# RWKV-7 chunk stage: the chunk output formed channel-major with 64 moving columns, its group norm taken by two products with a matrix of 1/64

## The chip, the core and the metric

The kernel runs on one core of one Trainium2 chip. The metric is the device time in microseconds (us) of one execution. TensorE is called PE below (PEld for its weight loads), VectorE DVE, ScalarE ACT, SyncE SP.

## What is computed

One decoder block on 2,064 tokens (16 meta tokens and 2,048 of the sequence) with 1,024 channels. Two branches start from one projection: an RWKV-7 time mixing on 512 channels (8 heads of 64) and an S5 state space model. Gates merge them, an output projection and a gated MLP with a causal convolution follow. The change lies in the RWKV branch, whose state S of each head runs over the tokens:

```python
def _rwkv7_step(S, inp):
    r_t, w_t, k_t, v_t, kk_t, b_t = inp
    sa = jnp.einsum('bhvk,bhk->bhv', S, -kk_t)
    S = S * w_t[:, :, None, :] + sa[..., None] * b_t[:, :, None, :] + v_t[..., None] * k_t[:, :, None, :]
    y = jnp.einsum('bhvk,bhk->bhv', S, r_t)
    return S, y
...
    mean = jnp.mean(y, axis=-1, keepdims=True)
    var = jnp.mean(jnp.square(y - mean), axis=-1, keepdims=True)
    y = ((y - mean) * lax.rsqrt(var + GN_EPS)).reshape(bsz, t_len, RWKV_WIDTH)
    y = y * ln_g.astype(f32) + ln_b.astype(f32)
```

The mean and the variance go over the 64 channels of a head, for each token.

## The kernel before

`hybrid_block` runs the stages one after the other: `norm_transpose` and `in_projection`, `rwkv_prepare`, `rwkv_chunks`, `branch_mix`, `token_projection`, `ffn_up` and `token_projection` again. The change is in `rwkv_chunks` alone (lines 999 to 1459) and in one table of masks that `lay_out` makes.

`rwkv_chunks` cuts the tokens into 33 chunks of 64 and turns the recurrence inside a chunk into matrix products. The 8 heads are 4 pairs (PAIRS); a pair fills the 128 partitions. Everything is float32, and each float32 product is two instructions on PE. The operands of a chunk are "roles" (A, B, K, R, V), loaded channel-major: the tile `roles` holds them block-diagonally, one head's 64 tokens in one half of the columns and the other's in the other half, with zeros elsewhere; the tile `pairs_ar` holds A and R compactly, 64 columns each.

The engines work through a software pipeline that is written out by hand. `steps` calls `step(c, ...)` for c = -1 to 32; the loop of the program holds two of these steps. In step c, PE, DVE and ACT finish chunk c (function names with `main_`), prepare chunk n = c + 1, and normalize chunk c - 1. In PE's order a step is:

- `grams_of` (L1122): the products of B and K with A and R, 128 columns each, into PSUM banks 0 and 1. DVE masks them (`mask_grams`, L1287 to L1297) into `l_t` and into three block-diagonal tiles `grams`.
- `turn_toks` (L1131): K, V and B are transposed; ACT copies them out (L1380).
- `main_u` (L1193): `u` of chunk c, in bank 5; ACT copies it (L1398). `turn_x1`, `main_m` (L1201, L1202) and on DVE `state` (L1313, L1315) update the state `m`.
- Five levels l = 0 to 4 of a triangular inverse. A level is `lx` (L1150) on PE, a masked copy `q` on DVE (L1302), `xq` (L1163, and L1165 in the last level) on PE, an addition into `x` on DVE (L1306, L1308), `turn_x` (L1172) on PE and a copy `x_t` on ACT (L1389), each in two halves of two pairs. Each waits for the one before it.

Into the waits of the levels the PE program puts other products, by the table `between`, whose keys are (level, place): place 0 is behind `lx`, 1 behind `xq`, 2 behind `turn_x`.

```python
between = {(0, 0): (ys, (0,)), (1, 0): (ys, (1,)), (1, 2): (ys, (2,)), (2, 0): (ys, (3,)),
           (2, 1): (ws, (0,)), (2, 2): (ws, (1,)), (3, 0): (ws, (2,)), (3, 1): (ws, (3,))}
```

`ys` is `main_y`: three products for each pair (L1212 to L1214), with block-diagonal R, or masked grams, as the stationary operand and the state, the tokens of V, or u as the moving one, so that y comes out with tokens on the partitions. `ws` is `main_w` for the next chunk (L1183, L1184). ACT copies y out of bank 7 (L1405). The norm of chunk c - 1 is on DVE behind levels 1, 2 and 3: `norm_mean` (a sum over the free axis, a scaling, a subtraction: L1323, L1325, L1327), `norm_squares` (L1331) and `norm_divide` (a reciprocal of 4 numbers in each partition, L1335, and two multiplications into the block-diagonal `y_bd`, L1340). ACT squares (L1409) and takes the root (L1413). In level 4, behind `lx`, PE transposes `y_bd` (`turn_y`, L1224), and ACT copies the result into `y_all` (L1419), which is channel-major. After the last chunk ACT applies the gain and bias (L1459), DVE adds the bonus and multiplies the gate (L1365, L1368), and the result is stored.

SP loads (`load_chunk`): for chunk c + 2, once `main_w` has released the buffers, A and R into `pairs_ar` (L1083), then B, K, A and V into `roles` (L1076), and once y is done R into `roles`.

## Time and profile before

| what | value |
|---|---|
| median of 3 runs | 4137.09 us (4135.92 to 4138.92) |
| the profiled execution: time | 4135.23 us |
| the profiled execution: span of the trace | 4133.5 us |
| mean granted TensorE clock | 0.957 of full speed |
| busy in the span: PE, PEld | 91%, 85% |
| busy in the span: DVE, ACT | 43%, 27% |

The span goes from the first to the last instruction of the trace; the execution's own time is 1.7 us longer. Matmuls overlap in PE's pipeline, so the busy time of PE says that something was in it, not that it was at its peak. Shares over the whole span mix eight stages; the change touches one, which lasts from about 1145 to 2040 us, and the rows quoted below are mostly of that stage. A row of the timeline gives the start, the time that the group took, the engine, the line, what is written and read, how many instructions, and in brackets the idle time of the engine before the group with what ended it. Successive instructions in a group of n on PE start (group time less the time of one) / (n - 1) apart.

### The profile page before, as it was taken

The numbers are of one execution on the slowest core, as the hardware profiler recorded it, in microseconds if no ns is written. First come the engines' busy times: TensorE is split into PE (matmuls) and PEld (weight loads), VectorE is DVE, ScalarE is ACT, GpSimd is POOL, SyncE is SP. The second block draws the span as 40 slices with busy tenths as digits, with TensorE's granted clock in tenths as the row PEclk, the third lists the DMA queues.
The fourth block names the chain that finished last, engine by engine and source line by source line (L and its number), as shares of the span: only waits on it lengthen the run. The fifth ranks groups of instructions, "written<-read, shape, count | busy, mean of one in ns | idle before, by whom it ended". The sixth has DMA issues, their size and how long they took to land. (4 is left out here: it accounts for less than half of the span.)

```text
span 4133.5 us, 61709 instructions
## 1 busy us (share of the span) xinstructions
PE 3778.9 (91%) x23380; PEld 3518.3 (85%) x23380; DVE 1784.3 (43%) x3099; ACT 1107.5 (27%) x1757; POOL 0.2 (0%) x4
## 2 busy tenths in 40 slices
PE   6999999995579999999499898999999999889899
PEld 6999999994468888888489887999999999878687
DVE  6556522224856666666554344322222222211233
ACT  5211133335523333333331133211111111111211
POOL 0000000000000000000000000000000000000000
PEclk8999999997689999999799999999999999999999
DMA  5333333434531111111443343111111111121333
GB/s 141 99 111 124 135 116 125 126 113 165 216 109 36 36 36 36 36 36 36 147 150 115 122 133 107 43 61 41 41 52 49 41 41 51 65 88 49 111 115 96
DMA packets 304699, 366.30 MB, mean 89 GB/s; under 512 B 167872, under 2 KB 250688, under 8 KB 292336
## 3 DMA queue, kind: packets, MB, share of 16 engines
q1 hardware_dynamic: 304624, 365.29, 28.2%
q8 instruction: 49, 0.80, 0.1%
q14 instruction: 26, 0.21, 0.0%
HBM read 225.97 MB, written 139.23 MB: 88 GB/s over the span
## 5 line engine op out<-in xcount | busy, mean ns | idle before, releaser
L2006 PE MATMUL psum<-h_hi,up_w_hi 128*128 128x344 f32 x2112 | 675.8, 320 | 15.2 <-DVE up_w_lo L2050 15.2
L2006 PE MATMUL psum<-h_lo,up_w_hi 128*128 128x344 f32 x2112 | 676.7, 320 | 0.0
L2006 PE MATMUL psum<-h_hi,up_w_lo 128*128 128x344 f32 x2112 | 674.5, 319 | 0.0
L434 PE MATMUL psum<-x_hi,proj_w_hi 128*128 128x344 f32 x1632 | 534.9, 328 | 9.3 <-DVE proj_w_lo L521 8.3
L434 PE MATMUL psum<-x_lo,proj_w_hi 128*128 128x344 f32 x1632 | 524.8, 322 | 0.0
L434 PE MATMUL psum<-x_hi,proj_w_lo 128*128 128x344 f32 x1632 | 523.7, 321 | 0.0
L2006 PEld LDWEIGHTS psum<-h_hi,up_w_hi 128*128 128x128 f32 x2112 | 397.7, 188 | 15.3 <-issue 15.3
L2006 PEld LDWEIGHTS psum<-h_hi,up_w_lo 128*128 128x128 f32 x2112 | 397.8, 188 | 0.0
L2006 PEld LDWEIGHTS psum<-h_lo,up_w_hi 128*128 128x128 f32 x2112 | 397.2, 188 | 0.0
L434 PEld LDWEIGHTS psum<-x_hi,proj_w_hi 128*128 128x128 f32 x1632 | 309.5, 190 | 11.0 <-issue 8.4
L1800 PE MATMUL psum<-down_w_hi,down_a_hi 128*128 128x512 f32 x704 | 278.8, 396 | 41.6 <-DVE down_w_lo L1920 30.2
L434 PEld LDWEIGHTS psum<-x_lo,proj_w_hi 128*128 128x128 f32 x1632 | 309.2, 189 | 1.4
L434 PEld LDWEIGHTS psum<-x_hi,proj_w_lo 128*128 128x128 f32 x1632 | 309.1, 189 | 0.0
L1800 PE MATMUL psum<-down_w_lo,down_a_hi 128*128 128x512 f32 x704 | 276.6, 393 | 0.0
L1800 PE MATMUL psum<-down_w_hi,down_a_lo 128*128 128x512 f32 x704 | 276.5, 393 | 0.0
L1581 PE MATMUL psum<-mix_y_hi,mix_w_hi 128*128 128x344 f32 x576 | 186.6, 324 | 61.3 <-DVE mix_y_lo L1634 61.3
L1389 ACT ACTIVATE chunk_x_t<-psum 128x256 f32<-128x256 f32 x264 | 95.0, 384 | 459.4 <-PE psum L1172 455.3
L2067 DVE TENSOR_SCALAR up_hidden<-up_a_pre,cols_sb 128x2048 f32<-128x2048 f32 x22 | 29.6, 1347 | 420.5 <-ACT up_a_pre L2035 420.5
L1800 PEld LDWEIGHTS psum<-down_w_hi,down_a_hi 128*128 128x128 f32 x704 | 133.9, 190 | 75.4 <-issue 20.3
L1302 DVE TENSOR_TENSOR chunk_q<-psum,chunk_masks 128x256 f32<-128x256 f32 x330 | 137.0, 423 | 122.8 <-PE psum L1150 119.9
L2077 DVE TENSOR_TENSOR up_hidden<-up_hidden,psum 128x328 f32<-128x328 f32 (+1 forms) x132 | 65.4, 509 | 288.8 <-PE psum L2006 243.1
L1150 PE MATMUL psum<-chunk_x,chunk_l_t 128*128 128x128 f32 x1320 | 181.4, 280 | 8.7 <-ACT chunk_x_t L1389 6.5
(290 smaller groups left out, 6231.1 us busy)
## 6 DMA issues: line engine op xcount, KB each, us to landing
up_weight<-in_w_up_tiles SPq DMA_DIRECT2D x22, 1024.0 KB, 4.9
scratch_hidden<-up_hidden SPq DMA_DIRECT2D x22, 1024.0 KB, 3.9
down_a_raw<-scratch_hidden SPq DMA_DIRECT2D x32, 704.0 KB, 5.0
proj_area<-scratch_s_tab SPq DMA_DIRECT2D x32, 608.5 KB, 3.7
scratch_s_tab<-proj_area SPq DMA_DIRECT2D x16, 1089.0 KB, 4.3
proj_weight<-in_w_in_tiles SPq DMA_DIRECT2D x34, 512.0 KB, 4.7
scratch_gates<-proj_mixed SPq DMA_DIRECT2D x16, 1032.0 KB, 4.4
mix_gate<-scratch_gates SPq DMA_DIRECT2D x32, 516.0 KB, 4.9
```

The lines of the kernel that those rows point to most:

```text
L434: mm = nc.tensor.matmul(psum[:, bank(v, n), 0:N_TOK], w[:, v, k, :], x[:, k, cols], start=(k == 0 and w is w_hi and x is x_hi), stop=(k == ...
L1150: mm = T_.matmul(half_bank(h)[:, n, :], l_t[:, 2 * h + j, :], x[:, 2 * h + j, :], start=True, stop=True)
L1302: V.tensor_tensor(q[:, js, :], half_bank(h), wide(3 + l, 2), ALU.mult).then_inc(q_ready, 1)
L1389: A.activation(x_t[:, v, js, :], half_bank(h), ACT.Copy).then_inc(xt_ready, 1)
L1581: mm = nc.tensor.matmul(psum[:, b, 0:N_TOK], w[:, u, part, k, :], y[:, src, k, cols], start=(k == 0 and w is w_hi and y is y_hi), stop=(k ...
L1800: mm = nc.tensor.matmul(psum[0:n, 2 * u + h, :], a[:, u, k, 0:n], w[:, k, h * HALF:(h + 1) * HALF], start=(k == 0 and a is a_hi and w is w ...
L2006: mm = nc.tensor.matmul(psum[:, bank(u, part, n), 0:N_TOK], w[:, u, part, k, :], y[:, k, block_cols(n)], start=(k == 0 and w is w_hi and y ...
L2067: nc.vector.tensor_scalar(out, tap(2), weight_of(2), conv_b[:, bass.ds(m, 1)], ALU.mult, ALU.add).then_inc(tap_done, 1)
L2077: nc.vector.tensor_tensor(cols, cols, psum[:, bank(u, 1, n), skip:N_TOK], ALU.mult).then_inc(b_used, 1)
```

## The change

- y is formed channel-major: the state, the tokens of V, and u are the stationary operands, 128 columns each; the moving operands are R and the masked grams, compact, 64 columns each. y comes out with channels on the partitions and 4 x 64 = 256 tokens on the free axis.
- R is held in `pairs_ar` alone. The block-diagonal load of R goes, and `pairs_ar` is now loaded after the four other roles and after the wait for y.
- The two masked grams that belong to R are kept in compact form (`gram_r`), made by one instruction on 128 partitions each in place of two on 64.
- The mean over a head is a product of y with a constant matrix that has 1/64 inside each head's block (`y_mean`, 256 moving columns, in bank 5), put behind `xq` of level 0; the variance is the same product of the squares (`y_var`), put behind `turn_x` and `main_w` of level 2. DVE subtracts the mean behind level 1. ACT takes the root of all 256 columns. DVE takes the reciprocal of all 256 columns and multiplies straight into `y_all` behind level 3.
- The sums over the free axis, the scaling, `turn_y` and the copy behind it go.

The diff, cut to its core:

```diff
+        gram_a = sb("gram_a", [P, 2, PAIRS, P])
+        gram_r = sb("gram_r", [P, 2, 2, PAIRS, S])
         toks = sb("toks", [P, 2, 3, PAIRS, P])
         pairs_ar = sb("pairs_ar", [P, 2, PAIRS, 2, S])
         l_t = sb("l_t", [P, PAIRS, P])
@@ -1027,10 +1029,9 @@
         w = sb("w", [P, PAIRS, P])
...
-        MASKED = 9
+        MASKED = 7
+        PLACE = {ROLE_A: 0, ROLE_B: 1, ROLE_K: 2, ROLE_V: 3}
+        incl = masks[:, MASK_INCL, 0:S].unsqueeze(1).broadcast_to([P, PAIRS, S])
+        head_mean = masks[:, MASK_MEAN, :]
+        y_bank = psum[:, 7, 0:PAIRS * S].rearrange("p (j c) -> p j c", j=PAIRS)
+        mean_bank = psum[:, 5, 0:PAIRS * S].rearrange("p (j c) -> p j c", j=PAIRS)
+        var_bank = psum[:, 5, PAIRS * S:2 * PAIRS * S].rearrange("p (j c) -> p j c", j=PAIRS)
...
                 if not isinstance(c, int) or c >= 2:
                     sp.wait_ge(w_done, c - 1)
-                for q, r in enumerate((ROLE_A, ROLE_R)):
-                    sp.dma_start(pairs_ar[:, v, :, q, S - n:S], prep[r][:, :, bass.ds(t0, n)].rearrange("j p t -> p j t")).then_inc(ar_loaded[v], 16)
                 for r in (ROLE_B, ROLE_K, ROLE_A, ROLE_V):
                     load(r, v, t0, n, roles_loaded)
                 if not isinstance(c, int) or c >= 2:
                     sp.wait_ge(y_done, c - 1)
-                load(ROLE_R, v, t0, n, r_loaded)
+                for q, r in enumerate((ROLE_A, ROLE_R)):
+                    sp.dma_start(pairs_ar[:, v, :, q, S - n:S], prep[r][:, :, bass.ds(t0, n)].rearrange("j p t -> p j t")).then_inc(ar_loaded[v], 16)
...
-                at(pe, masked, MASKED, c, 3)
-                at(pe, masked, MASKED, c, MASKED - 4)
+                at(pe, masked, MASKED, c, 4)
...
-                done(pe, y_flat, 2, c)
+                at(pe, std_done, 1, c, 1)
...
-            def main_y(c, v, k, pairs):
+            def main_y(c, v, pairs):
                 if pairs[0] == 0:
                     at(pe, u_ready, 1, c, 1)
-                    pe.wait_ge(r_loaded[v], 32 * k + 32)
-                    done(pe, y_ready, 2, c)
+                    done(pe, y_ready, 1, c)
                 for j in pairs:
-                    T_.matmul(bank(7)[:, j, :], R(v, ROLE_R, j), m[:, v, j, :], start=True, stop=False)
-                    T_.matmul(bank(7)[:, j, :], grams[:, v, 2, j, :], toks[:, v, 2, j, :], start=False, stop=False)
-                    mm = T_.matmul(bank(7)[:, j, :], grams[:, v, 1, j, :], u[:, j, :], start=False, stop=True)
+                    T_.matmul(y_bank[:, j, :], m[:, v, j, :], pairs_ar[:, v, j, 1, :], start=True, stop=False)
+                    T_.matmul(y_bank[:, j, :], toks[:, v, 2, j, :], gram_r[:, v, 1, j, :], start=False, stop=False)
+                    mm = T_.matmul(y_bank[:, j, :], u[:, j, :], gram_r[:, v, 0, j, :], start=False, stop=True)
                 if pairs[-1] == PAIRS - 1:
                     mm.then_inc(y_done, 1)
 
-            def turn_y(c):
-                at(pe, normed, 2, c, 2)
+            def y_mean(c):
+                at(pe, y_ready, 1, c, 1)
                 at(pe, u_ready, 1, c, 2 if not isinstance(c, int) or c < NC_ - 1 else 1)
-                if isinstance(c, int) and c == NC_ - 1:
-                    at(pe, y_flat, 2, c, 2)
-                for j in range(PAIRS):
-                    mm = T_.transpose(bank(5)[:, j, :], y_bd[:, j].rearrange("p h c -> p (h c)"), ident)
-                mm.then_inc(y_turned, 1)
+                at(pe, std_done, 1, c, 2)
+                T_.matmul(mean_bank, head_mean, y[:], start=True, stop=True).then_inc(mean_done, 1)
+
+            def y_var(c):
+                at(pe, sq_ready, 1, c, 1)
+                T_.matmul(var_bank, head_mean, y_sq[:], start=True, stop=True).then_inc(var_done, 1)
...
+                    norm = main and not (isinstance(c, int) and c == 0)
+                    mean, var = (lambda: norm and y_mean(c - 1)), (lambda: norm and y_var(c - 1))
+                    between = {(0, 0): (ys, (0,)), (0, 1): (mean, ()), (2, 3): (var, ()), (1, 0): (ys, (1,)), (1, 2): (ys, (2,)), (2, 0): (ys, (3,)),
...
-            V.memset(y_bd[:], 0.0).then_inc(eps_set, 1)
...
-                mask_product(grams[:, v, 1], 0, 1, 1)
+                V.tensor_tensor(gram_r[:, v, 0], product(0, 1), incl, ALU.mult).then_inc(masked, 1)
                 at(dve, grams_done, 2, c, 2)
-                mask_product(grams[:, v, 0], 1, 0, 0)
-                mask_product(grams[:, v, 2], 1, 1, 1)
+                mask_product(gram_a[:, v], 1, 0, 0)
+                V.tensor_tensor(gram_r[:, v, 1], product(1, 1), incl, ALU.mult).then_inc(masked, 1)
...
-            def norm_mean(c):
-                at(dve, y_ready, 2, c, 2)
-                V.tensor_reduce(stat[:, 0, :], y[:], mybir.AxisListType.X, ALU.add).then_inc(norm_own, 1)
-                at(dve, norm_own, OWN, c, 1)
-                V.tensor_scalar(stat[:, 0, :], stat[:, 0, :], 1.0 / HEAD_DIM, None, ALU.mult).then_inc(norm_own, 1)
-                at(dve, norm_own, OWN, c, 2)
-                V.tensor_tensor(y[:], y[:], wide_stat(0), ALU.subtract).then_inc(norm_own, 1)
-
-            def norm_squares(c):
-                at(dve, sq_ready, 1, c, 1)
-                V.tensor_reduce(stat[:, 1, :], y_sq[:], mybir.AxisListType.X, ALU.add).then_inc(norm_own, 1)
+            def norm_center(c):
+                at(dve, mean_done, 1, c, 1)
+                at(dve, y_ready, 1, c, 1)
+                V.tensor_tensor(y[:], y[:], mean_bank, ALU.subtract).then_inc(centered, 1)
 
             def norm_divide(c):
-                at(dve, std_done, 1, c, 1)
-                V.reciprocal(stat[:, 3, :], stat[:, 2, :]).then_inc(norm_own, 1)
-                at(dve, norm_own, OWN, c, 5)
-                at(dve, y_turned, 1, c, 1)
-                for h in range(2):
-                    rows = slice(h * 64, (h + 1) * 64)
-                    V.tensor_tensor(y_bd[rows, :, h, :], y[rows], wide_stat(3)[rows], ALU.mult).then_inc(normed, 1)
+                at(dve, std_done, 1, c, 3)
+                V.reciprocal(y_std[:], y_std[:]).then_inc(inverted, 1)
+                at(dve, inverted, 1, c, 1)
+                V.tensor_tensor(y_all[:, :, bass.ds(c * S, S)], y[:], y_std[:], ALU.mult).then_inc(normed, 1)
...
-                    norms = [norm_mean, norm_squares, norm_divide]
+                    norms = {1: norm_center, 3: norm_divide}
...
+            act.sem_inc(std_done, 2)
...
-                done(act, normed, 2, c)
-                for h in range(2):
-                    rows = slice(h * 64, (h + 1) * 64)
-                    A.activation(y[rows], bank(7)[rows, :, h * 64:(h + 1) * 64], ACT.Copy).then_inc(y_ready, 1)
+                done(act, normed, 1, c)
+                A.activation(y[:], y_bank, ACT.Copy).then_inc(y_ready, 1)
...
-                at(act, norm_own, 5, c, 3)
+                at(act, centered, 1, c, 1)
                 A.activation(y_sq[:], y[:], ACT.Square).then_inc(sq_ready, 1)
 
             def deviation(c):
-                at(act, norm_own, 5, c, 4)
-                A.activation(stat[:, 2, :], stat[:, 1, :], ACT.Sqrt, scale=1.0 / HEAD_DIM, bias=eps[:]).then_inc(std_done, 1)
-
-            def y_flat_out(c):
-                at(act, y_turned, 1, c, 2)
-                for h in range(2):
-                    rows = slice(h * 64, (h + 1) * 64)
-                    A.activation(y_all[rows, :, bass.ds(c * S, S)], bank(5)[rows, :, h * 64:(h + 1) * 64], ACT.Copy).then_inc(y_flat, 1)
-            act.sem_inc(y_flat, 2)
-            act.sem_inc(y_turned, 1)
+                at(act, var_done, 1, c, 1)
+                done(act, normed, 1, c)
+                A.activation(y_std[:], var_bank, ACT.Sqrt, bias=eps[:]).then_inc(std_done, 1)
...
+    masks += [(head[None, :] == 0) & (r <= c), same / HEAD_DIM]
```

At two places the rows of the engines' programs show where the new work stands; in both, steps in the middle of the loop are shown. The first is PE from `xq` of level 0 to `lx` of level 1. Before:

```order
L1163 MATMUL psum<-chunk_q,chunk_x_t 128x128 x2
L1050 REGISTER_ALU
L1163 MATMUL psum<-chunk_q,chunk_x_t 128x128 x2
L1172 MATMUL psum<-ident_sb,chunk_x 128x128 x4
L1050 ISA
L1150 MATMUL psum<-chunk_x,chunk_l_t 128x128 x2
```

and in the changed kernel:

```order
L1168 MATMUL psum<-chunk_q,chunk_x_t 128x128 x2
L1057 REGISTER_ALU
L1168 MATMUL psum<-chunk_q,chunk_x_t 128x128 x2
L1226 MATMUL psum<-chunk_y,chunk_masks 128x256
L1177 MATMUL psum<-ident_sb,chunk_x 128x128 x4
L1057 ISA
L1155 MATMUL psum<-chunk_x,chunk_l_t 128x128 x2
```

The product for the mean stands between `xq` and `turn_x`, where nothing stood. The one for the variance, further on in the same program, stands between `main_w` and `lx` of level 3:

```order
L1177 MATMUL psum<-ident_sb,chunk_x 128x128 x4
L1188 MATMUL psum<-chunk_toks,chunk_gram_a 128x128
L1189 MATMUL psum<-chunk_m,chunk_roles 128x128
L1230 MATMUL psum<-chunk_y_sq,chunk_masks 128x256
L1057 REGISTER_ALU
L1155 MATMUL psum<-chunk_x,chunk_l_t 128x128 x2
```

Without L1230, whose place was empty, these rows read the same before. The second place is DVE between level 3 and level 4. Before:

```order
L1306 TENSOR_TENSOR chunk_x<-chunk_x,psum 128x256 x2
L1335 RECIPROCAL chunk_stat<-chunk_stat 128x4
L1050 REGISTER_ALU
L1340 TENSOR_TENSOR chunk_y_bd<-chunk_y,chunk_stat 64x4x64 x2
L1050 REGISTER_ALU
L1302 TENSOR_TENSOR chunk_q<-psum,chunk_masks 128x256
```

and in the changed kernel:

```order
L1312 TENSOR_TENSOR chunk_x<-chunk_x,psum 128x256 x2
L1331 RECIPROCAL chunk_y_std<-chunk_y_std 128x256
L1333 ISA
L1333 TENSOR_TENSOR chunk_y_all<-chunk_y,chunk_y_std 128x4x64
L1057 REGISTER_ALU
L1308 TENSOR_TENSOR chunk_q<-psum,chunk_masks 128x256
```

The reciprocal goes from 4 to 256 elements in each partition, at the same place ahead of level 4.

## Rows read from the trace of the kernel before

**Rows 1.** Source line of `main_u`, once a step in steps 0 to 32: first and last start.

```profile
L1193 PEld LDWEIGHTS psum<-chunk_w,chunk_x_t x264: 186/192/192, 1185.6 to 1998.6; 128*128 128x128 f32 x132
```

**Rows 2.** Windows: busy of PE, PEld, DVE, ACT, POOL, clock, DMA share, GB/s.

```profile
1186.00:1996.00 810.00, 768.99 (x6230) 698.65 (x6229) 524.96 (x1234) 263.20 (x632) 0.00 (x0) 1.00 0.17 35
```

**Rows 3.** Timeline of PE in a later step, from `lx` of level 1 to that of level 2.

```profile
1601.08 1.16 PE L1150 MATMUL psum<-chunk_x,chunk_l_t 128*128 128x128 f32 x8
...
1602.74 1.06 PE L1163 MATMUL psum<-chunk_q,chunk_x_t 128*128 128x128 f32 x8
...
1605.26 1.06 PE L1150 MATMUL psum<-chunk_x,chunk_l_t 128*128 128x128 f32 x8
```

**Rows 4.** The same in step -1, in which no `main_y` is issued.

```profile
1169.20 1.13 PE L1150 MATMUL psum<-chunk_x,chunk_l_t 128*128 128x128 f32 x8
...
1172.63 1.13 PE L1150 MATMUL psum<-chunk_x,chunk_l_t 128*128 128x128 f32 x8
```

**Rows 5.** Source lines: duration of one in ns, least, median and greatest.

```profile
L1150 PEld LDWEIGHTS psum<-chunk_x,chunk_l_t x1320: 186/192/192, 1165.7 to 1995.6; 128*128 128x128 f32 x189
L1150 PE MATMUL psum<-chunk_x,chunk_l_t x1320: 275/275/377, 1165.8 to 1995.7; 128*128 128x128 f32 x189
...
L1172 PE MATMUL psum<-ident_sb,chunk_x x528: 272/273/332, 1168.2 to 1994.3; 128*128 128x128 f32 x176
...
L392 PEld LDWEIGHTS psum<-proj_area x64: 92/97/146, 123.9 to 490.9; 128*16 128x16 f32 x64
```

**Rows 6.** Timeline of PE in `rwkv_prepare`: float32 products with 256 moving columns.

```profile
1027.23 1.89 PE L850 MATMUL psum<-prep_work,prep_heads 128*128 128x256 f32 x8
```

**Rows 7.** Timeline in level 0 of the next step: `xq`, `turn_x`, `x_t`.

```profile
1624.48 1.15 PE L1163 MATMUL psum<-chunk_q,chunk_x_t 128*128 128x128 f32 x8 [0.45 <-DVE chunk_q L1302]
...
1625.70 0.20 PEld L1172 LDWEIGHTS psum<-ident_sb,chunk_x 128*128 128x128 f32 x2 [0.26 <-DVE chunk_x L1306]
...
1626.17 0.83 ACT L1389 ACTIVATE chunk_x_t<-psum 128x256 f32<-128x256 f32 x2 [5.31 <-PE psum L1172]
```

**Rows 8.** Timeline from level 2 to level 3.

```profile
1608.58 0.67 ACT L1389 ACTIVATE chunk_x_t<-psum 128x256 f32<-128x256 f32 x2 [2.88 <-PE psum L1172]
...
1609.12 1.06 PE L1150 MATMUL psum<-chunk_x,chunk_l_t 128*128 128x128 f32 x8
```

**Rows 9.** Timeline from level 3 to level 4, DVE and PE.

```profile
1611.11 0.87 DVE L1306 TENSOR_TENSOR chunk_x<-chunk_x,psum 128x256 f32<-128x256 f32 x2 [0.47 <-PE psum L1163]
...
1612.10 0.87 DVE L1340 TENSOR_TENSOR chunk_y_bd<-chunk_y,chunk_stat 64x256 f32<-64x256 f32 x2
...
1613.40 0.87 DVE L1302 TENSOR_TENSOR chunk_q<-psum,chunk_masks 128x256 f32<-128x256 f32 x2 [0.44 <-PE psum L1150]
...
1613.65 0.60 PE L1224 MATMUL psum<-ident_sb,chunk_y_bd 128*128 128x128 f32 x4
...
1614.09 1.06 PE L1165 MATMUL psum<-chunk_x_t,chunk_q 128*128 128x128 f32 x8
```

**Rows 10.** Groups by line: busy us, mean ns of one, idle before.

```profile
L530 DVE TENSOR_TENSOR proj_area<-proj_area 128x32 f32<-128x32 f32 x82 | 11.1, 188 | 1.0
...
L1335 DVE RECIPROCAL chunk_stat<-chunk_stat 128x4 f32<-128x4 f32 x33 | 5.6, 171 | 0.7 <-ACT chunk_stat L1413 0.7
...
L589 DVE RECIPROCAL proj_area<-proj_area 128x32 f32<-128x32 f32 x1 | 0.4, 353 | 0.0
```

**Rows 11.** DMA issues from 1187 to 1979 us: count, KB, median us to landing.

```profile
chunk_pairs_ar<-scratch_roles SPq DMA_DIRECT2D x60, 128.0 KB, 2.4
```

**Rows 12.** Timeline: two memsets at the stage's start, which come before the first loads.

```profile
1146.78 0.48 DVE L1265 MEMSET chunk_y_bd<- 128x512 f32 x1
...
1147.76 2.19 DVE L1268 MEMSET chunk_roles<- 128x2560 f32 x1 [0.48 <-DVE chunk_eps L1266]
```

**Rows 13.** Timeline of the last step: the first product of y, and the gain.

```profile
1999.63 0.49 PE L1212 MATMUL psum<-chunk_m,chunk_roles 128*128 128x128 f32 x2 [0.69 <-ACT chunk_u L1398]
...
2008.88 8.10 ACT L1459 ACTIVATE chunk_y_all<-chunk_y_all,cols_sb 128x2064 f32<-128x2064 f32 x4
```

74 lines of the change are left out of this document (33 added, 41 removed).

## The prediction, as put on record before the changed kernel ran

> **What bounds the kernel now.** I read the page's first part first (its shares stand in the table above): PE is busy for 91% of the span, so the time is PE's, but a share over eight stages says nothing of the one that changes. Next came the windows: between 1186 and 1996 us PE is busy for 769 of 810 us at the full granted clock, DVE for 525, ACT for 263, and the DMA engines for a sixth of it [rows 2]. `main_u` comes once a step, and its first and last starts lie 813 us and 32 steps apart: 25.4 us a step [rows 1]. So PE is nearly full, but "busy" includes matmuls that wait in its pipeline; what bounds a step has to be read off the timeline.
>
> The timeline shows a chain, `lx` on PE, `q` on DVE, `xq` on PE, `x` on DVE, `turn_x` on PE, `x_t` on ACT, which goes round in five levels, with PE issuing other products in the gaps. A level without `main_y` takes 1172.63 - 1169.20 = 3.43 us [rows 4]. A level with two of the four pieces of `main_y` takes 1605.26 - 1601.08 = 4.18 us [rows 3]. The two pieces are 12 instructions. From the row of 8, (1.06 - 0.275) / 7 = 0.112 us lie between the starts of two [rows 3, 5], so the pieces issue for 1.34 us and 0.75 of it is exposed: the first half of a piece fills a wait, the second half delays the chain. Therefore PE work inside a level is worth about half of its issue time if added or removed in a gap, and all of it where the gap is already full. And DVE work is free only while it fits between an `x` and the next `q`.
>
> **y with 64 columns moving.** 4 pairs x 3 products x 2 instructions = 24 instructions per step keep their number; the moving side halves. No row has a float32 product with 128 columns loaded and 64 moving, so I bound it. Low: the moving side sets the pace, 0.112 / 2 = 0.056 us. High: load and movement one after the other, 0.102 + 0.056 = 0.158 us. What can be read is the load. The first matmul after a wait, with nothing to hide its load, takes 377 ns against 275: the load of 128 float32 columns takes 102 ns. For a transpose it is 332 - 272 = 60 ns. And a float32 load of 16 columns lasts 97 ns against 192 for 128, that is 0.85 ns for a column, 109 ns for 128 [rows 5]. So a load takes as long as 128 columns take to move twice; the two overlap now and both fit in 0.112 us. With half the movement the load still needs 0.102 to 0.109 us. I take 0.112 us, no change, **0 us**. At the low bound the pieces in places (1, 0), (1, 2) and (2, 0) would give back 6 x 0.056 = 0.33 us each, 1.0 us a step; the piece in (0, 0) gives nothing, since PE already waits 0.45 us behind it for `q`, which DVE starts after `state` [rows 7]. At the high bound they would cost 18 x 0.046 = 0.8 us.
> The Trainium skill, "TensorE: Matmul & The Clock Gate", section "LDWEIGHTS (loading the stationary operand)", gives a load as columns / 1.2 ns, 107 ns for 128 columns: the trace agrees (102, 109). The same page's section "Back-to-back issue gap" speaks the other way: a gap of N / 2.4 + 2.5 ns, which for two passes of 64 columns would be 56 ns; that is the first rival below.
>
> **The mean product** is two instructions of 256 columns. In the row with 256 columns the starts lie (1.89 - 0.33) / 7 = 0.22 us apart, taking 0.33 for the last one [rows 6], so it issues for 0.44 us. It stands between `xq` and `turn_x` of level 0, where PE waits 0.26 us for `x` ahead of each half [rows 7]. `xq` is issued by 1624.48 + 0.89 = 1625.37; with the mean PE is free at 1625.81 instead of turning the first half at 1625.70. The second half waits for its `x` until 1626.14 anyway, after which ACT is 0.10 us late. **+0.12 us**; bounds 0 and 0.44.
>
> **The variance product** issues for 0.44 us too, behind `main_w` of level 2. There PE is the late one: ACT has both halves of `x_t` ready at 1608.58 + 0.67 = 1609.25, and the first half before `lx` starts at 1609.12, its second half being issued at 1609.56 [rows 8]. No wait is left to fill: **+0.44 us**; bounds 0.2 and 0.44.
>
> **DVE between levels 3 and 4.** Before: `x` ends at 1611.11 + 0.87 = 1611.98, a reciprocal of 4 elements and two multiplications end at 1612.97, and `q` starts at 1613.40 when `lx` allows. DVE has 1.42 us there and uses 0.99 [rows 9]. Afterwards it takes the reciprocal of 256 elements and one multiplication of 0.42 (half of the 0.87 for two). The price of that reciprocal is not in the trace. For 4 elements it is 171 ns, for 32 it is 353, while an ordinary instruction with 32 takes 188 [rows 10]. Bounds: 0.42 us if it cost what every other DVE instruction on 128x256 does; 256 x 353 / 32 = 2.82 us if all of the 353 ns were per element. The straight line through the two rows, (353 - 171) / 28 = 6.5 ns for an element, gives 353 + 224 x 6.5 = **1.81 us**, and I take it, as the two rows that share its operation give it. The block is then 1.81 + 0.42 + two gaps of 0.03 = 2.29 us.
> The chain up to `x` of level 3 is 0.56 us late by the two products, so the block ends at 1611.98 + 0.56 + 2.29 = 1614.83. `q` of half 0 ends 0.45 later, and `xq` can start 0.05 behind it, at 1615.33. Before, it was issued at 1613.98 (0.11 ahead of 1614.09), because `turn_y`, issued from 1613.54 on, came first; DVE alone, with its first half of `q` ready at 1613.82, would have allowed 1613.87. So `turn_y`, 4 instructions, is worth only 0.11 us, and that is already within the difference: 1615.33 - 1613.98 = 1.35 us, of which 0.12 + 0.44 are the products and **+0.79 us** the reciprocal.
>
> **What costs nothing.** The masks of R, two DVE instructions fewer and 0.87 us, lie where DVE is ahead: `lx` of level 0 follows `main_m`, on which PE is busy. `norm_center` takes 0.42 us where three instructions of 1.0 were. The two copies that ACT loses, and its root of 256 columns (some 0.42 in place of 0.29), lie in ACT's two thirds of idle time [rows 2]; y's copy on ACT now waits for the reciprocal and pushes `w` to some 1615.9, which `main_u` needs only after grams and transposes, 4 us after `xq`. On SP two loads go; `pairs_ar` is now loaded behind the wait for y, at about 1607 instead of a level earlier in the step before. It lands 2.4 us later [rows 11], and the grams need it at 1615; without these 5 us of cover the lateness would stand in front of the grams in full.
>
> **Sum.** 31 steps have a norm (c = 1 to 31): 31 x 1.35 = +41.9 us. The start: the memset of `y_bd` (0.48) and a fifth of that of `roles` (0.44) go ahead of the first loads [rows 12]: -0.9. The tail: from the first product of y to the gain it was 9.25 us [rows 13]. Now, after 2.7 us of products, come twice over a mean (0.55), centring (0.42), squares (0.42), variance (0.55), root (0.42), reciprocal (1.81) and multiplication (0.42), with handovers of 0.05 each and y's copy (0.42) between the two: 12.6 us, +3.4. Together +44.4, which from the profiled execution's 4135.2 gives 4179.6. That execution was 1.9 us under the median of three, well inside what repeats; against the median it is 4181.5. I put down **4180 us**.
>
> **Rivals.**
> 1. *Movement sets the pace of y* (0.056 us at 64 columns). For it: movement and load tie now, so the rows can't show which one binds. Against it: the 102 and 109 ns of the load. It gives 31 x 1.0 and 1.3 in the tail: 4180 - 32 = 4148. Chance 0.12.
> 2. *The other side: new shapes cost by elements streamed.* If an element costs what it costs elsewhere, on PE and on DVE, the reciprocal takes 0.42 us, the block 0.9, and it fits the 1.42 us ahead of level 4 again. It decides there: below about 0.97 us for the reciprocal DVE is no longer late, and `turn_y`'s 0.11 counts as gain. A step is then 0.12 + 0.44 - 0.11 - 1.0 = -0.55 us, the tail 3.4 - 2.8 - 1.3: 4137 - 17 - 0.9 - 0.7 = 4118. Against it: 353 against 188 ns at 32 elements. Chance 0.06.
> 3. *A cheap reciprocal alone*, y unchanged: 31 x 0.45 - 0.9 + 0.6 = +14, 4151. Chance 0.04.
> 4. *A dearer reciprocal*: part of the 171 ns for 4 elements is fixed time that hides the elements, so that the slope is steeper. With eight times the ordinary 1.03 ns for an element ((0.42 - 0.188) / 224) it is 2.27 us: 31 x 0.46 + 0.9 = +15, 4195. Chance 0.14. The Trainium skill, "VectorE: DVE Perf Modes", section "First, the fixed hardware budget", says that the reciprocal divides iteratively with a repeat count of 8; the trace's two rows make it 6.3 times.
>
> **Chances and range.** The forecast has 0.64. Its own uncertainty (0.105 to 0.12 us for y, the shares of the two products) is 4165 to 4190. Faster or slower by 0.2%, 8.3 us, is about what a measurement of this kernel can tell. Faster needs rival 2: 0.07. Same takes the edge of rivals 1 and 3, which lie 3 to 6 us above the border: 0.04. Slower: 0.89. The range leaves out rival 2 and the worst of the reciprocal's upper bound, and reaches from rival 1 to rival 4: 4147 to 4199.
>
> **What would show it.** A step of 26.7 us. LDWEIGHTS of y's products still starting about 0.11 us apart, in groups of six no shorter than now. The reciprocal at about 1.8 us, then `q` of level 4 no longer released by `lx`, and PE idle for over 1 us ahead of `xq` of level 4, with DVE's `q` named as releaser. `lx` of level 3 some 0.56 us later against level 0 than now. Wrong would be: y's instructions 0.06 us apart, a reciprocal near 0.4 us, or an idle PE ahead of the grams with a DMA as its releaser.

## The result, and the profile of the changed kernel

| | before | changed |
|---|---|---|
| median of three runs, us | 4137.09 (4135.92 to 4138.92) | 4175.52 (4173.19 to 4180.03) |
| profiled execution, us | 4135.23 | 4180.03 |
| span of the trace, us | 4133.5 | 4178.3 |

The changed kernel is slower: ratio 1.0094, 95% interval 1.0071 to 1.0117. The forecast was 4180 us in 4147 to 4199, with 0.89 for slower. So the sign, the time and the mechanism came out; the working is gone through term by term below. That the profiled execution took just 4180.03 us is chance: 3.4 us of its distance to the one before lie in stages that were not changed, as shown below.

Window of the changed kernel, the stretch of [rows 2] (busy of PE, PEld, DVE, ACT, POOL, clock, DMA share, GB/s):

```profile
1186.00:1996.00 810.00, 742.93 (x5959) 677.18 (x5958) 475.16 (x1001) 217.99 (x515) 0.00 (x0) 1.00 0.14 29
```

All engines are busy for less of the same 810 us than before: PE 743 against 769, DVE 475 against 525, ACT 218 against 263 [rows 2]. But fewer steps fit into them now, so that this doesn't say how much work a step has. Windows over the same 14 steps do (1312.86 to 1669.51 us before, 1290.75 to 1664.10 us changed):

| 14 steps, busy us (instructions) | before | changed |
|---|---|---|
| time | 356.65 | 373.35 |
| PE | 338.67 (2747) | 342.18 (2746) |
| PEld | 307.76 (2745) | 312.05 (2745) |
| DVE | 232.33 (547) | 219.99 (463) |
| ACT | 116.87 (281) | 100.91 (239) |

In a step DVE is relieved of 0.9 us and ACT of 1.1, while PE has as many instructions as before and 0.25 us more busy time: four instructions with 256 moving columns stand in the place of the four transposes of `turn_y`. The step got 1.2 us longer. A sum of busy time doesn't explain that; the chain does. The pace is read from `main_u`, as in [rows 1], now on line 1198:

```profile
L1198 PEld LDWEIGHTS psum<-chunk_w,chunk_x_t x264: 186/192/193, 1185.5 to 2035.1; 128*128 128x128 f32 x132
```

849.6 us over 32 steps is 26.55 us a step, where it was 813.0 / 32 = 25.41. In the middle of the loop, where every step has a norm, the 14 steps take 373.35 us (1290.75 to 1664.10) against 356.65 (1312.86 to 1669.51): 26.67 against 25.48, +1.19 us. Where does it stand? First level 0, timeline of the changed kernel (start, us, engine, line, operation; in brackets the idle time before it and its releaser):

```profile
1643.42 1.15 PE L1168 MATMUL psum<-chunk_q,chunk_x_t 128*128 128x128 f32 x8 [0.50 <-DVE chunk_q L1308]
...
1644.41 0.60 PE L1226 MATMUL psum<-chunk_y,chunk_masks 128*128 128x256 f32 x2
...
1644.84 0.68 PE L1177 MATMUL psum<-ident_sb,chunk_x 128*128 128x128 f32 x4
1645.26 0.68 ACT L1383 ACTIVATE chunk_x_t<-psum 128x256 f32<-128x256 f32 x2 [5.47 <-PE psum L1177]
1645.70 0.97 PEld L1155 LDWEIGHTS psum<-chunk_x,chunk_l_t 128*128 128x128 f32 x8 [0.41 <-ACT chunk_x_t L1383]
```

`turn_x` has no wait ahead of it any more; the product fills the one of 0.26 us in [rows 7] and the like one of the second half. From `xq` to `lx` it takes 1645.70 - 1643.42 = 2.28 us, where it was 2.13 (1624.48 to 1626.61). **+0.15.** Then from level 2 to level 3:

```profile
1625.33 0.87 DVE L1312 TENSOR_TENSOR chunk_x<-chunk_x,psum 128x256 f32<-128x256 f32 x2 [0.69 <-PE psum L1168]
...
1626.44 0.67 ACT L1383 ACTIVATE chunk_x_t<-psum 128x256 f32<-128x256 f32 x2 [3.10 <-PE psum L1177]
...
1626.97 0.60 PE L1230 MATMUL psum<-chunk_y_sq,chunk_masks 128*128 128x256 f32 x2
1627.19 1.08 PEld L1155 LDWEIGHTS psum<-chunk_x,chunk_l_t 128*128 128x128 f32 x8
...
1628.05 0.87 DVE L1308 TENSOR_TENSOR chunk_q<-psum,chunk_masks 128x256 f32<-128x256 f32 x2 [1.86 <-PE psum L1155]
```

ACT has the whole `x_t` ready at 1627.11, and `lx` is loaded only at 1627.19, behind the variance product: PE is the late one, as before [rows 8]. From `x` of level 2 to `q` of level 3 it takes 1628.05 - 1625.33 = 2.72 us, where it was 2.30 (1607.47 to 1609.77). **+0.42.** Then from level 3 to level 4:

```profile
1629.39 0.87 DVE L1312 TENSOR_TENSOR chunk_x<-chunk_x,psum 128x256 f32<-128x256 f32 x2 [0.47 <-PE psum L1168]
...
1630.18 1.75 DVE L1331 RECIPROCAL chunk_y_std<-chunk_y_std 128x256 f32<-128x256 f32 x1
...
1630.94 1.16 PE L1155 MATMUL psum<-chunk_x,chunk_l_t 128*128 128x128 f32 x8 [0.19 <-ACT chunk_x_t L1383]
1632.07 0.42 DVE L1333 TENSOR_TENSOR chunk_y_all<-chunk_y,chunk_y_std 128x256 f32 x1
1632.42 0.75 DVE L1308 TENSOR_TENSOR chunk_q<-psum,chunk_masks 128x256 f32<-128x256 f32 x2
...
1632.89 1.16 PE L1170 MATMUL psum<-chunk_x_t,chunk_q 128*128 128x128 f32 x8 [0.79 <-DVE chunk_q L1308]
```

Before, `q` followed the start of `lx` by 0.75 us (1612.65 to 1613.40, [rows 9]); here that would be 1631.69, but `q` starts at 1632.42, when DVE is through with the norm. It has no releaser in its row: it followed its own engine. PE waits for it in every step, in the waits of this kernel between 1190 and 2020 us (us in total, times, longest):

```profile
PEld psum L1170 <- DVE chunk_q L1308: 29.6, 31, 1.0
PE psum L1170 <- DVE chunk_q L1308: 23.6, 30, 0.8
```

From the first `x` to `xq` of level 4 it now takes 1632.89 - 1629.39 = 3.50 us, where it was 1613.98 - 1611.11 = 2.87. **+0.63.** The three make 1.20 us and the middle of the loop shows 1.19, so nothing of size is left elsewhere in the step.

y itself gave nothing. One of its lines, all products of the program:

```profile
L1217 PEld LDWEIGHTS psum<-chunk_gram_r,chunk_toks x264: 191/192/193, 1190.2 to 2038.5; 128*128 128x128 f32 x132
L1217 PE MATMUL psum<-chunk_gram_r,chunk_toks x264: 274/276/276, 1190.3 to 2038.6; 128*128 128x64 f32 x132
```

The load takes its 192 ns as in [rows 5] and the product 276 against 275, with half the columns moving. Its pairs start 0.22 us apart (1622.34, 1622.56, 1622.79), 0.11 for an instruction as before. The load of `pairs_ar`, issued later, is covered: it goes out at 1624.82 and the grams start at 1633.95 with no wait for a DMA.

The tail, timeline from the mean of the last chunk but one to the gain:

```profile
2038.91 0.65 PE L1226 MATMUL psum<-chunk_y,chunk_masks 128*128 128x256 f32 x2
...
2044.51 0.96 PE L1226 MATMUL psum<-chunk_y,chunk_masks 128*128 128x256 f32 x2 [3.29 <-ACT chunk_y L1397]
...
2046.43 1.22 PE L1230 MATMUL psum<-chunk_y_sq,chunk_masks 128*128 128x256 f32 x2 [0.96 <-ACT chunk_y_sq L1401]
...
2048.19 1.75 DVE L1331 RECIPROCAL chunk_y_std<-chunk_y_std 128x256 f32<-128x256 f32 x1 [2.27 <-ACT chunk_y_std L1406]
...
2050.44 8.10 ACT L1440 ACTIVATE chunk_y_all<-chunk_y_all,cols_sb 128x2064 f32<-128x2064 f32 x4 [2.28 <-DVE chunk_y_all L1333]
```

From the first product of y (2036.18) to the gain it takes 14.26 us against 9.25 [rows 13]: +5.0.

The account of the profiled executions: `main_u` starts at 1185.5 against 1185.6 (-0.1), the loop adds 849.6 - 813.0 = +36.6, the tail +5.0, together +41.5; `branch_mix` issues its first load at 2083.95 against 2042.52, +41.4. The remaining 3.4 of the 44.8 us fall into stages whose code is the same, and this execution is the slowest of the three of the changed kernel; by the medians the difference is 38.4.

### The profile page after: what moved, and what is told of

Same layout as the page of the kernel before. It is cut to its first block and busy times, and to the rows that moved or that the text cites. A ratio compares the mean times of both kernels' runs of the same rounds, so it can differ in the third digit from the quotient of the medians.

```text
span 4178.3 us, 60968 instructions
## 1 busy us (share of the span) xinstructions
PE 3791.8 (91%) x23380; PEld 3531.5 (85%) x23380; DVE 1752.3 (42%) x2900; ACT 1070.2 (26%) x1658; POOL 0.2 (0%) x4
## 5 line engine op out<-in xcount | busy, mean ns | idle before, releaser
L1155 PEld LDWEIGHTS psum<-chunk_x,chunk_l_t 128*128 128x128 f32 x1320 | 162.7, 192 | 30.5 <-ACT chunk_x_t L1383 25.1
```

What stands on the lines that cost most here:

```text
L1155: mm = T_.matmul(half_bank(h)[:, n, :], l_t[:, 2 * h + j, :], x[:, 2 * h + j, :], start=True, stop=True)
```

## The experiments

All kernels start from the changed one, except where it is said. "Pace" is the first and last start of `main_u` divided by 32, as above. The kernel before ran beside each and took 4140 to 4142 us there, 2 to 5 us more than in the table above, so paces say more than differences of medians. Ratios are to the kernel before. The two kernels that ran once have no interval.

### y with 128 moving columns

```diff
-        gram_r = sb("gram_r", [P, 2, 2, PAIRS, S])
+        gram_r = sb("gram_r", [P, 2, 2, PAIRS, 2, S])
...
-                    T_.matmul(y_bank[:, j, :], m[:, v, j, :], pairs_ar[:, v, j, 1, :], start=True, stop=False)
+                    T_.matmul(y_bank[:, j, :], m[:, v, j, :], pairs_ar[:, v, j].rearrange("p q c -> p (q c)"), start=True, stop=False)
```

(and the same for the other two products; the masked grams are written to the upper 64 columns of each pair, the lower ones hold zeros, and the copy takes the upper ones.)

> The changed kernel with 128 moving columns in y's products again (the compact operands are preceded by 64 columns that only fill up; y is still channel-major). Theory, the load of 128 float32 columns sets the pace of y's products: nothing changes, a step stays at 26.55 us within 0.05, the time within 3 us of the changed kernel's 4175.5. Rival, the 64 columns do save something that the later waits hide: a step gets up to 1.0 us longer, 4206.

Measured: 4178.67 us (4173.73 to 4181.54), ratio 1.0097 (1.0080 to 1.0114), pace 26.56. The source line of one product of y:

```profile
L1217 PE MATMUL psum<-chunk_gram_r,chunk_toks x264: 275/275/275, 1187.9 to 2036.5; 128*128 128x128 f32 x132
```

Doubling the moving columns changes neither the product nor the pace (26.56 against 26.55). The 64 saved columns were worth nothing.

### y with 64 loaded columns

```diff
-                    T_.matmul(y_bank[:, j, :], m[:, v, j, :], pairs_ar[:, v, j, 1, :], start=True, stop=False)
+                    T_.matmul(y_bank[0:64, j, :], m[:, v, j, 0:64], pairs_ar[:, v, j, 1, :], start=True, stop=False)
```

(and the same for the other two; y of the upper 64 channels of each pair is left out, and ACT copies 64 partitions.)

> The changed kernel with only half of the stationary columns loaded in y's products: 64 loaded, 64 moving; y of the upper 64 channels of each pair is left out. If the load sets the pace, the starts of y's instructions move from 0.113 to about 0.056 us apart, each piece of six issues for 0.34 instead of 0.67 us, and a step gets 1.0 us shorter (three exposed pieces), some 31 us in all: 4145. If a fixed issue time of about 0.1 us for each matmul sets it, the starts stay 0.11 us apart and nothing changes.

Measured, one run: 4183.10 us, pace (2038.3 - 1187.3) / 32 = 26.59. Timeline of this kernel, level 1:

```profile
1621.44 0.97 PEld L1155 LDWEIGHTS psum<-chunk_x,chunk_l_t 128*128 128x128 f32 x8 [0.41 <-ACT chunk_x_t L1384]
...
1622.53 0.19 PEld L1216 LDWEIGHTS psum<-chunk_pairs_ar,chunk_m 128*64 128x64 f32 x2
...
1622.64 0.20 PEld L1217 LDWEIGHTS psum<-chunk_gram_r,chunk_toks 128*64 128x64 f32 x2
...
1622.76 0.20 PEld L1218 LDWEIGHTS psum<-chunk_gram_r,chunk_u 128*64 128x64 f32 x2
...
1623.02 0.97 PEld L1168 LDWEIGHTS psum<-chunk_q,chunk_x_t 128*128 128x128 f32 x8
```

Pairs now start 0.11 us apart, 0.057 for an instruction, and one load takes 138 ns instead of 192. So the load sets the pace of a float32 product with 128 loaded columns: halving it too halves the distance, halving the movement alone doesn't, and a fixed issue time of 0.1 us for each instruction is excluded. The Trainium skill, "TensorE: Matmul & The Clock Gate", section "LDWEIGHTS (loading the stationary operand)", gives a load as columns / 1.2 ns, by which 64 columns are an estimate of 53 ns. The trace is near it with 57 ns, but 64 columns move here as well, so the 57 ns are no measurement of the load alone.

But the step gained nothing, and that was not expected. The eight loads of `lx` take 0.89 us, so the next should start at 1622.33; it starts at 1622.53. And the last of y should be followed 0.057 us later, at 1622.87; `xq` comes at 1623.02. Entering and leaving the narrower form costs 0.20 + 0.15 us, as much as the six instructions save (0.33).

### One product of three with 64 loaded columns

```diff
-                    T_.matmul(y_bank[:, j, :], toks[:, v, 2, j, :], gram_r[:, v, 1, j, :], start=False, stop=False)
+                    T_.matmul(y_bank[0:64, j, :], toks[:, v, 2, j, 0:64], gram_r[:, v, 1, j, :], start=False, stop=False)
```

(The tokens' product is left out for the upper 64 channels of each pair.)

> The changed kernel with 64 loaded columns in the middle one of the three products of each pair of y only (so for the upper 64 channels the tokens' product is left out), 128 in the other two. In e2_y_load64 the six instructions of a piece gave back 6 x 0.056 = 0.34 us and the gaps at its two ends, from 128 loaded columns to 64 and back, took it again: 0.20 and 0.14 us. Theory, each change of the width costs that wherever it stands: two of six instructions give back 0.11 and the two changes take 0.34, so each of the three exposed pieces gets 0.23 longer and a step 0.7 us, 27.2 us. Rival, the gaps of e2 came from its place in the chain and not from the width: a step of 26.2 to 26.5 us.

Measured, one run: 4199.99 us, pace (2053.4 - 1186.9) / 32 = 27.08, with fewer columns loaded than in the changed kernel. The timeline of its level 0:

```profile
1625.11 0.30 PEld L1216 LDWEIGHTS psum<-chunk_pairs_ar,chunk_m 128*128 128x128 f32 x2
...
1625.48 0.19 PEld L1217 LDWEIGHTS psum<-chunk_gram_r,chunk_toks 128*64 128x64 f32 x2
...
1625.74 0.30 PEld L1218 LDWEIGHTS psum<-chunk_gram_r,chunk_u 128*128 128x128 f32 x2
```

Without a loss the pairs would start at 1625.33 and 1625.44. The last pair starts 1625.74 - 1625.44 = 0.30 us late. This piece lies in a wait; the exposed piece of level 1 shows the same distances and takes 1630.52 - 1629.67 = 0.85 us up to `xq`, where the changed kernel's takes 1624.57 - 1623.90 = 0.67. Three such pieces make 0.54 us, and 0.53 were measured (0.7 were expected, with 0.23 for a piece). So the loss comes with a change of form also in the middle of y's products, away from `lx` and `xq`. Whether it is the loaded columns or the output's 64 partitions that cause it stays open: both change together here.

### The reciprocal of 4 columns

```diff
-                V.reciprocal(y_std[:], y_std[:]).then_inc(inverted, 1)
+                V.reciprocal(y_std[:, :, 0:1], y_std[:, :, 0:1]).then_inc(inverted, 1)
```

> The changed kernel with the reciprocal of 4 of the 256 columns only; the rest of the norm's division is left out. Theory, the 1.75 us reciprocal is 0.63 us of each step and 1.6 us at each of its two places in the tail: a step of 25.9 us, 4175.5 - 31 x 0.63 - 3 = 4153. Rival, PE's order is what holds level 4 and the reciprocal only fills the wait: under 5 us change.

Measured: 4157.15 us (4151.33 to 4158.56), ratio 1.0040 (1.0026 to 1.0055), pace 25.91. Less the changed kernel's 26.55 that is -0.64, what the timeline gave for the reciprocal (0.63). In this kernel's timeline `x` of level 3 to `xq` of level 4 takes 1623.10 - 1620.33 = 2.77 us, 0.10 less than before, as `turn_y` is gone; but the grams follow 1.13 us behind `xq` (1624.23) in place of 1.06, which takes most of that back.

### Without the two products of the statistics

```diff
-                T_.matmul(mean_bank, head_mean, y[:], start=True, stop=True).then_inc(mean_done, 1)
+                pe.sem_inc(mean_done, 1)
...
-                T_.matmul(var_bank, head_mean, y_sq[:], start=True, stop=True).then_inc(var_done, 1)
+                pe.sem_inc(var_done, 1)
```

(ACT takes the root of the squares instead of the variance. The norm's mean and variance are left out.)

> The changed kernel without its two products with the matrix of 1/64; the norm's mean and variance are left out (DVE and ACT read what lies there). Theory: 0.15 us for the mean and 0.43 for the variance go from a step, 26.0 us, but the block of DVE behind level 3 stays as long: 4175.5 - 31 x 0.58 - 1 = 4157. If only their issue time counted, 0.88 us a step would go: 4147. If they lay in waits, nothing.

Measured: 4154.49 us (4152.24 to 4159.31), ratio 1.0038 (1.0024 to 1.0052), pace 25.99: -0.56, where the timeline gave 0.15 + 0.42. The two differences add up to 1.20 us, which would leave 25.35, the pace of before (25.41) within 0.06. So nothing of size is missing from the account. No kernel leaves out the reciprocal and the products at once, so that the shares add up is not shown by itself.

### The variance product in another place

```diff
-                    between = {(0, 0): (ys, (0,)), (0, 1): (mean, ()), (2, 3): (var, ()), (1, 0): (ys, (1,)), (1, 2): (ys, (2,)), (2, 0): (ys, (3,)),
+                    between = {(0, 0): (ys, (0,)), (0, 1): (mean, ()), (1, 1): (var, ()), (1, 0): (ys, (1,)), (1, 2): (ys, (2,)), (2, 0): (ys, (3,)),
...
-                    norms = {1: norm_center, 3: norm_divide}
+                    norms = {0: norm_center, 3: norm_divide}
```

(`norm_center` goes behind level 0, and ACT's squares and root go one level ahead too.)

> The changed kernel with the mean subtracted behind level 0, the squares taken there, and the variance product moved from behind main_w of level 2, where PE is late, to between xq and turn_x of level 1, where PE waits 0.26 us for x as it does in level 0. Theory, the place sets its price: 0.15 us as for the mean instead of 0.43, a step of 26.27 us, 4175.5 - 31 x 0.28 = 4167. Rival, the product costs its 0.44 us wherever it stands: no change.

Measured: 4169.35 us (4161.35 to 4173.90), ratio 1.0068 (1.0045 to 1.0091), pace 26.14. That is -0.41 where -0.28 was expected. The timeline of this kernel at the new place:

```profile
1617.05 0.97 PEld L1168 LDWEIGHTS psum<-chunk_q,chunk_x_t 128*128 128x128 f32 x8
...
1618.06 0.60 PE L1230 MATMUL psum<-chunk_y_sq,chunk_masks 128*128 128x256 f32 x2
...
1619.57 0.41 PEld L1155 LDWEIGHTS psum<-chunk_x,chunk_l_t 128*128 128x128 f32 x3
```

and the same place in the changed kernel:

```profile
1620.49 0.97 PEld L1168 LDWEIGHTS psum<-chunk_q,chunk_x_t 128*128 128x128 f32 x8
...
1621.72 0.20 PEld L1177 LDWEIGHTS psum<-ident_sb,chunk_x 128*128 128x128 f32 x2 [0.26 <-DVE chunk_x L1312]
...
1622.17 0.20 PEld L1177 LDWEIGHTS psum<-ident_sb,chunk_x 128*128 128x128 f32 x2 [0.25 <-DVE chunk_x L1312]
...
1623.01 0.97 PEld L1155 LDWEIGHTS psum<-chunk_x,chunk_l_t 128*128 128x128 f32 x8
```

Both take 2.52 us from `xq` to `lx`. The product of 0.44 us fits whole into the two waits of 0.26 and 0.25 us, and here a piece of y stands behind `turn_x`, so that PE, not ACT's copy, decides when `lx` starts. In level 0 no piece stands there and ACT decides, which is why the mean costs 0.15. A product of the same size is worth 0.42, 0.15 or nothing, by its place.

### The same, and the reciprocal in two halves

```diff
-            def norm_divide(c):
+            def norm_invert(c):
                 at(dve, std_done, 1, c, 3)
-                V.reciprocal(y_std[:], y_std[:]).then_inc(inverted, 1)
-                at(dve, inverted, 1, c, 1)
+                V.reciprocal(y_std[:, 0:2], y_std[:, 0:2]).then_inc(inverted, 1)
+
+            def norm_divide(c):
+                V.reciprocal(y_std[:, 2:4], y_std[:, 2:4]).then_inc(inverted, 1)
+                at(dve, inverted, 2, c, 2)
...
-                    norms = {0: norm_center, 3: norm_divide}
+                    norms = {0: norm_center, 2: norm_invert, 3: norm_divide}
```

> As e5_var_early, and the reciprocal cut in two of 128 columns, one behind level 2 and one, with the multiplication, behind level 3; the whole computation is done. Theory: 0.93 us fits the gap of DVE of 1.4 us behind level 2, 0.93 + 0.42 just fits the one behind level 3, so the 0.63 us go and nearly all of the change's loss with them: a step of 25.6 to 25.7 us, 4147. Rival, DVE's order counts and not the gaps: the two halves together cost more than the whole, over 4167.

Measured: 4148.42 us (4142.10 to 4151.37), ratio 1.0021 (1.0011 to 1.0030), pace 25.49. DVE's timeline of this kernel, levels 2 to 4:

```profile
1607.47 0.94 DVE L1331 RECIPROCAL chunk_y_std<-chunk_y_std 128x128 f32<-128x128 f32 x1
1608.99 0.87 DVE L1308 TENSOR_TENSOR chunk_q<-psum,chunk_masks 128x256 f32<-128x256 f32 x2 [0.57 <-PE psum L1155]
...
1611.11 0.95 DVE L1334 RECIPROCAL chunk_y_std<-chunk_y_std 128x128 f32<-128x128 f32 x1
1612.20 0.43 DVE L1336 TENSOR_TENSOR chunk_y_all<-chunk_y,chunk_y_std 128x256 f32 x1
1612.62 0.87 DVE L1308 TENSOR_TENSOR chunk_q<-psum,chunk_masks 128x256 f32<-128x256 f32 x2
```

The first half fits between `x` and `q` with 0.57 us to spare, so it costs nothing. The second, with the multiplication, ends just as `q` can start: from `x` (1610.33) to `q` 2.29 us, as in [rows 9] (1611.11 to 1613.40). Of the 1.14 us that the change costs in a step 1.06 are back, without a change to y or to what is computed: the loss was one of places. The kernel is still 9 us slower than the one before, of which the longer tail, with both halves in it, has over 5.

### The kernel before, with its products spread

Starting from the kernel before, `main_y` and `main_w` are cut into single products (twelve and eight) and laid one or two to a wait, but for three behind `lx` of level 0:

```diff
-                    between = {(0, 0): (ys, (0,)), (1, 0): (ys, (1,)), (1, 2): (ys, (2,)), (2, 0): (ys, (3,)),
-                               (2, 1): (ws, (0,)), (2, 2): (ws, (1,)), (3, 0): (ws, (2,)), (3, 1): (ws, (3,))}
+                    between = {(0, 0): ((ys, (0, 1, 2)),), (0, 1): ((ys, (3,)),), (0, 2): ((ys, (4,)),), (1, 0): ((ys, (5,)),), (1, 1): ((ys, (6, 7)),), (1, 2): ((ys, (8, 9)),), (2, 0): ((ys, (10,)),), (2, 1): ((ys, (11,)), (ws, (0,)),), (2, 2): ((ws, (1, 2)),), (3, 0): ((ws, (3,)),), (3, 1): ((ws, (4, 5)),), (3, 2): ((ws, (6, 7)),)}
```

> The kernel before with main_y cut into its 12 products and main_w into its 8, spread one or two at a time over the places behind lx, xq and turn_x of levels 0 to 3. Theory, a wait in a level holds some 0.3 us of other PE work and what goes beyond delays the chain: the three pieces of 0.67 us cost 0.34 each now and products of 0.22 us cost next to nothing, a step of 24.2 to 24.5 us, 4137 - 32 x 1.0 = 4105. Rival, PE's total issue time bounds a step: no change.

Measured: 4105.36 us (4102.21 to 4112.46), ratio 0.9915 (0.9896 to 0.9934), pace 24.41. PE in level 1 of this kernel:

```profile
1614.75 0.97 PEld L1150 LDWEIGHTS psum<-chunk_x,chunk_l_t 128*128 128x128 f32 x8
...
1615.75 0.39 PE L1215 MATMUL psum<-chunk_u,chunk_grams 128*128 128x128 f32 x2
1615.98 0.97 PEld L1163 LDWEIGHTS psum<-chunk_q,chunk_x_t 128*128 128x128 f32 x8
...
1618.28 0.86 PEld L1150 LDWEIGHTS psum<-chunk_x,chunk_l_t 128*128 128x128 f32 x7
```

The level takes 1618.28 - 1614.75 = 3.53 us, by loads, where it was 4.07 (1601.08 to 1605.15), and 3.43 with nothing in it at all [rows 4]. Five products stand in this level now where there were six; in the whole step PE does exactly the same work in both kernels. The median is the lowest of the study, under both the kernel before and the changed one.

### Both together

The kernel with the split reciprocal, and its products spread by a table of its own: four of y and the mean product stand behind `lx` of level 0, the variance product alone behind `xq` of level 1, and the others one or two to a wait as far as the first of level 4.

> As e6_early_split, with main_y and main_w spread product by product as in e7_before_spread. Theory: the gains add up, a step of 24.0 to 24.5 us, some 4100, under both kernels. Rival, the mean and variance products of 0.44 us and the half reciprocals leave no room for the others: a step of over 25 us.

Measured: 4110.89 us (4101.14 to 4116.86), ratio 0.9929 (0.9904 to 0.9954), pace (1967.8 - 1188.3) / 32 = 24.36. The step is as expected, the time 11 us over the 4100 that were. Against the one before it the intervals overlap; the step is the same within 0.05 us and the longer tail stays (14.55 us from 1968.91 to the gain at 1983.46). Once the products stand in the waits, no difference between the channel-major form and what the kernel before does can be told.

## Why the prediction was right, point by point

| term | predicted | measured | by |
|---|---|---|---|
| y with 64 moving columns, a step | 0 | 0 | the experiment with 128 |
| mean product | +0.12 | +0.15 | timeline |
| variance product | +0.44 | +0.42 | timeline; both products 0.56 by leaving them out |
| reciprocal | +0.79 | +0.63 | timeline; 0.64 with 4 columns |
| the loop | +41.9 | +36.6 | first and last `main_u` |
| the start | -0.9 | -0.1, and -0.7 within the stage | first `main_u` |
| the tail | +3.4 | +5.0 | first product of y to the gain |
| sum | +44.4 | +41.5 | the stage alone |

**The bound of the step** was right: a chain round the levels, for which PE's busy share says nothing. DVE and ACT got less to do and PE 0.25 us more in a step, and the step got 1.2 us longer; that PE's total doesn't set it, the kernels with the variance product moved and with the products spread show, since both are faster with the same work. One reading in the working was off without entering the sum: the 4.18 us of a level run from a first product with its load ahead of it to one whose load had started 0.11 us earlier. By loads it is 4.07 (1601.08 to 1605.15), so 0.64 us of the two pieces are exposed and not 0.75. One sign was missed by a little: PE stands idle ahead of `xq` of level 4 for 0.79 us, its loads for 0.98, where over 1 us was put down.

**y at no gain** was right and for the stated reason. The load of 128 float32 columns (102 to 109 ns by [rows 5]) already fills nearly all of the 0.112 us between two instructions; fewer moving columns leave the load. The rival by which movement sets the pace is excluded by the two experiments on y: twice the movement costs nothing, and the distance halves only when the load is halved too. The formula that the prediction set against this is given by the Trainium skill, "TensorE: Matmul & The Clock Gate", section "Back-to-back issue gap", for a single product by itself, and the section says that at few columns it comes out too low, as it has no room for the load. So that page didn't speak the other way.

**The two products** were right within 0.03 us, because their price was read from the wait at their place.

**The reciprocal** was the term mis-sized most in the loop, 0.16 us of 0.79. Its straight line through two small rows held: 1.746 us against 1.81, and 0.945 for 128 elements, so (1.746 - 0.945) / 128 = 6.3 ns for an element, where the line had 6.5. The dearer reciprocal of 2.27 us and the cheap one of 0.42 are excluded. The Trainium skill, "VectorE: DVE Perf Modes", section "First, the fixed hardware budget", has a repeat count of 8; 6.3 over the 1.03 ns of an ordinary element is 6.1, so here the measurement differs from that reading of it. What the term missed is how neighbours follow each other on DVE. From `x` to `xq` it added up to 0.87 + 0.03 + 1.81 + 0.03 + 0.42 + 0.45 + 0.05 = 3.66 us. Measured are 0.79 (the reciprocal starts 0.08 ahead of the end of `x`, which it doesn't need), 1.75, then 0.14 ahead of the multiplication, which does need it (in the tail it is 0.03, so that isn't a price of the dependence alone), 0.35 to `q`, which doesn't, and 0.47 to `xq`: 3.50.

**The start** was right, and the small difference of the first `main_u` is chance. From the start of the stage `main_u` comes 39.3 us later (1146.16 to 1185.5), where it was 40.1 (1145.53 to 1185.6): 0.7 us less. The stage itself started 0.6 us later in this execution, which has nothing to do with the change. The other runs bear this out: from the load of the masks, which opens the stage, to `main_u` it is 38.9 to 39.5 us in the eight experiments that start from the changed kernel and 40.0 in the spread kernel before (1150.75 to 1190.7), while the start of the stage lies anywhere from 1143.9 to 1150.8.

**The tail** was the largest error beside its size: +5.0 for +3.4. The working took 0.55 us for each of the four products of the statistics; they lasted 0.65, 0.70, 0.96 and 1.22, 1.33 us more together. In the last two the granted clock was down: windows of the changed kernel (columns as above),

```profile
2039.00:2042.00 3.00, 1.26 (x5) 0.46 (x4) 0.66 (x2) 0.89 (x2) 0.00 (x0) 1.00 0.00 0
2042.00:2045.00 3.00, 0.49 (x2) 0.30 (x2) 1.94 (x2) 0.38 (x1) 0.00 (x0) 0.97 0.00 0
2045.00:2046.40 1.40, 0.47 (x2) 0.00 (x0) 0.42 (x1) 0.42 (x1) 0.00 (x0) 0.50 0.00 0
2046.40:2048.00 1.60, 1.22 (x2) 0.50 (x2) 0.00 (x0) 0.31 (x1) 0.00 (x0) 0.50 0.00 0
```

0.50 is 1.2 GHz, and from 2039 to 2045 us, up to about its fall, PE had been busy for 1.8 of 6 us. The tail of before had the same fall (0.50 from 2006.9 to 2008.1 us), but there only the last `turn_y` met it, with 1.12 us where it takes 0.60 in the loop. The first two products lost 0.25 us to the working at the full clock. Moving the norm onto PE put PE on the path of a stretch in which it is mostly idle, and that was not in the sum. The handovers took 0.65 us in all, where 0.3 had been allowed: fifteen operations follow one another, and the working counted fewer.

**What cancels.** The median rose by 38.4 us and the stage by 41.5 in the profiled executions; the sum said 44.4. The errors in the step and the tail have opposite signs, so the total is closer than its parts, the loop being 5.3 us too long and the tail 1.6 too short. That closeness is luck.

## What to carry to other kernels

Ask of a product which side paces it before making one side smaller: a float32 product with 128 columns freshly loaded lies 0.11 us behind the last one whether 64 or 128 columns move, and what a narrower load gave back (0.33 us for six instructions) was eaten by the changes of form around it (0.35). In a chain of waits, work is priced by its place, not by its length: a product of 0.44 us cost 0.42, 0.15 or nothing, a 1.75 us reciprocal cost 0.63 whole and nearly nothing in halves, and the same twenty products, mostly one or two to a wait in place of whole pieces, made the step 1.0 us shorter, with no work removed. Compare busy time over the same number of steps and not over the same time: the second made PE's work look smaller when it had grown. And when a step gets longer by more than any engine's work, look for what stands between two links of the chain and is longer than its gap (here the reciprocal in 1.4 us on DVE, and the variance product where PE had no wait).

## What the hardware showed that was not expected

- Between float32 products with 128 and with 64 loaded columns (and 128 and 64 output partitions) PE loses 0.15 to 0.21 us on entering the narrower form and 0.14 to 0.15 on leaving it, in two kernels and at several places, as far as one run of each can show.
- A DVE instruction that doesn't depend on the one ahead of it starts 0.07 to 0.09 us before that one's end. The multiplication, which reads the reciprocal's result, starts 0.14 us after its end in the loop (1630.18 + 1.75 to 1632.07) but 0.03 after it in the tail (2041.77 + 1.75 to 2043.55). In the loop a register operation of 64 ns stands ahead of it, in the tail none; whether that makes the difference is not shown.
- A reciprocal of 128x256 float32 takes 1.746 us, of 128x128 0.945, 6.3 ns for an element in each partition, where 256 elements of another DVE instruction take 0.42 us.
